# Rotation of queries and keys by position: halves of heads swapped by GpSimd's loads inside SBUF in place of rotation products on TensorE

## The reference, cut to what matters

```python
def apply_rope(x, cos, sin):
    xf = x.astype(jnp.float32)
    x1, x2 = jnp.split(xf, 2, axis=-1)
    c = cos[:, None, :]
    s = sin[:, None, :]
    return jnp.concatenate([x1 * c - x2 * s, x2 * c + x1 * s], axis=-1).astype(x.dtype)

def even_mixer(...):
    a_q, a_k, a_v, b_q, b_k, b_v, i_q, i_k, i_w = jnp.split(h @ w_in, EVEN_SPLITS, axis=-1)
    a_q = apply_rope(...cos64, sin64)      # and a_k: 8 heads of 64
    o_a = diff_attention(a_q, a_k, a_v, lam, subln, lambda_init)
    b_q = apply_rope(...cos64, sin64)      # and b_k: 8 heads of 64
    i_q = apply_rope(...cos32, sin32)      # 8 index heads of 32, and i_k: one of 32
    o_b = dsa_attention(b_q, b_k, b_v, i_q, i_k, i_w, topk)   # each query keeps its 64 best keys by index score
    return jnp.concatenate([o_a, o_b], axis=-1) @ w_out
```

## Time and profile before

| | |
|---|---|
| time, median of 3 runs | 1786.7 us (1786.68 to 1788.54) |
| the profiled execution's own time | 1785.52 us |
| its span | 1783.7 us |
| PE busy | 1715.3 us (96%) |
| DVE busy | 1159.3 us (65%) |
| ACT busy | 894.3 us (50%) |
| POOL busy | 7.4 us |
| the stretch from `idx` to the end of attention "even" | about 955 to 1080 us |

### The profile page before, as it was taken

The page is one execution under the profiler, slowest core; times in us unless marked ns, Lnnn a source line. Parts: engine busy times, 40 slices in busy tenths (PEclk is TensorE's granted clock), DMA queues, the critical chain, the costliest instruction groups (busy, mean ns, idle before and its releaser), DMA issues.

```text
span 1783.7 us, 22030 instructions
## 1 busy us (share of the span) xinstructions
PE 1715.3 (96%) x8926; PEld 1431.7 (80%) x8926; DVE 1159.3 (65%) x1613; ACT 894.3 (50%) x1271; POOL 7.4 (0%) x20
## 2 busy tenths in 40 slices
PE   5999999999989999999999989999999999999998
PEld 4798788888867888888888867888888889778887
DVE  7779888789766754565547967555655456675553
ACT  3555544465567444554444556444544445574432
POOL 0000000000000000000000000000000000000000
PEclk9999999999999999999999999999999999999999
DMA  8957677766624664555554324545555556345451
GB/s 355 401 228 274 266 298 289 297 253 245 259 77 186 234 224 177 200 197 177 185 195 178 119 71 177 182 169 192 201 188 177 184 207 225 116 153 182 169 192 47
DMA packets 54117, 363.43 MB, mean 204 GB/s; under 512 B 5744, under 2 KB 8944, under 8 KB 13056
## 3 DMA queue, kind: packets, MB, share of 16 engines
q1 hardware_dynamic: 52256, 351.47, 53.7%
q0 software_dynamic: 1760, 10.56, 1.5%
HBM read 360.95 MB, written 1.05 MB: 203 GB/s over the span
## 4 chain that ended last, share of the span: by engine, by line
PE 80%; DVE 12%; DMA 3%; ACT 3%; issue 1%; SPq 0%; POOL 0%; DVEq 0%; ACTq 0%
PE pp L603 77%; DVE low L1796 4%; DVE raw L1809 2%; DMA raw<-in_w 2%; PE pp L853 2%; DMA cst<-in_csts 1%; PE pp L785 1%; ACT wh L1270 1%; DVE hf L1940 1%; PE pp L930 1%; DVE tb L1796 1%; DVE x L1799 0%; DVE hl L1796 0%; DVE Sb L2091 0%; DVE sc L2192 0%
## 5 line engine op out<-in xcount | busy, mean ns | idle before, releaser
L1796 DVE TENSOR_TENSOR low<-raw,wh 128x2048 fp32r<-128x2048 f32 (+3 forms) x340 | 638.0, 1890 | 360.2 <-ACT wh L1270 359.8
L1270 ACT ACTIVATE wh<-raw 128x2048 fp32r<-128x2048 f32 (+3 forms) x346 | 536.1, 1567 | 436.3 <-PE pp L603 292.3
L603 PE MATMUL pp<-wh,hh 128*128 128x512 f32 x1312 | 522.0, 398 | 12.0 <-ACT hh L1300 6.7
L603 PE MATMUL pp<-low,hh 128*128 128x512 f32 x1312 | 514.6, 392 | 7.1 <-DVE low L1796 6.9
L603 PE MATMUL pp<-wh,hl 128*128 128x512 f32 x1312 | 507.3, 392 | 3.8 <-DVE hl L1796 3.8
L603 PEld LDWEIGHTS pp<-wh,hh 128*128 128x128 f32 x1312 | 247.7, 189 | 69.8 <-issue 16.0
L603 PEld LDWEIGHTS pp<-low,hh 128*128 128x128 f32 x1312 | 248.2, 189 | 58.6 <-DVE low L1796 9.8
L603 PEld LDWEIGHTS pp<-wh,hl 128*128 128x128 f32 x1312 | 247.6, 189 | 57.6 <-DVE hl L1796 5.1
L603 PE MATMUL pp<-wh,hidh 128*128 128x512 f32 x592 | 232.1, 392 | 0.0
L603 PE MATMUL pp<-low,hidh 128*128 128x512 f32 x592 | 230.6, 389 | 1.0 <-DVE low L1796 1.0
L603 PE MATMUL pp<-wh,hidl 128*128 128x512 f32 x592 | 230.6, 389 | 0.0
(11 more groups left out here) (207 smaller groups left out, 1159.6 us busy)
## 6 DMA issues: line engine op xcount, KB each, us to landing
raw<-in_w SPq DMA_DIRECT2D x314, 1024.0 KB, 4.8
raw<-in_w SPq DMA_DIRECT2D x24, 768.0 KB, 4.3
gain<-in_w POOLq DMA_DIRECT2D x6, 512.0 KB, 4.5
bT<-in_rel POOLq DMA_DIRECT2D x1, 2048.0 KB, 11.4
cst<-in_csts POOLq DMA_DIRECT2D x1, 1029.0 KB, 19.8
xT<-in_xT SPq DMA_DIRECT2D x1, 1024.0 KB, 7.4
binr<-in_bin POOLq DMA_DIRECT2D x1, 1024.0 KB, 10.9
wsT<-in_ws POOLq DMA_DIRECT2D x1, 1024.0 KB, 15.2
```

The costliest lines, as they stand in the source:

```text
L603: return e.matmul(out, lhsT, rhs, start=start, stop=stop, skip_group_check=True)
L1270: q.then_inc(e.activation(wh[j % NW][:, c], raw[i % NRAW][:, c], ACT.Copy), s_wh, (j, part))
L1796: return e.tensor_tensor(out, a, b, op)
```

## The change

The two rotation matrices leave the constants. The sine table takes the sign (minus in the first half of each head). PE's `rope` and its five calls are gone. POOL gets a function `turn_halves`: for each of the five groups it waits for ACT's copy, then moves each half of each head from `ta` to the place of the other half in `tb`, by one load inside SBUF for each block of partitions. That is 8 loads of 16 partitions x 3 KB for `idx`, and 4 loads of 32 partitions x 4 KB for each of the others, 24 in all. DVE's sine product reads `tb` in place of PSUM, in one instruction for all tiles, after it has waited for all loads of the group. On POOL the five calls stand between `gain_row("even_out", "dn2")` and `gain_row("dn3", "even_out")`.

```diff
-CSTS = [("ident", 128), ("bd64", 128), ("rot64", 128), ("rot32", 128), ("cos64", 256),
+CSTS = [("ident", 128), ("bd64", 128), ("cos64", 256),
         ("sin64", 256), ...
...
-        return np.cos(ang).astype(np.float32)[rows], np.sin(ang).astype(np.float32)[rows]
+        sign = np.where(p % d < d // 2, np.float32(-1), np.float32(1))[:, None]
+        return np.cos(ang).astype(np.float32)[rows], np.sin(ang).astype(np.float32)[rows] * sign
...
+        TURNS = {("idx", 0): (16, 3), ("aqk", 0): (32, 4), ("aqk", 1): (32, 4), ("bqk", 0): (32, 4), ("bqk", 1): (32, 4)}
+        s_turned = {key: signal("turned_%s%d" % key) for key in TURNS}
...
# tensor_program
-            def rope(key, kind, nt, ring):
-                q.wait_ge(s_sq, (key,))
-                small_tiles(key, ring, C("rot" + kind), ta.of((key,)),
-                            lambda n: tuple(range(2 * n, min(nt, 2 * n + 2))), (s_side, key))
...
             def idx_rest():
-                rope(("rope", "idx", 0), "32", 3, misc)
+                q.wait_ge(s_sq, (("rope", "idx", 0),))
...
-                if (qb, jj) == (1, 0):
-                    rope(("rope", "aqk", 0), "64", 4, misc)
...
-                if n == 1:
-                    rope(("rope", "aqk", 1), "64", 4, t_r)
...
-                    rope(("rope", "bqk", g), "64", 4, t_r)
...
# vector_program
-            def rope(name, gi, kind, nt, dst, scale, ring=misc):
+            def rope(name, gi, kind, nt, dst, scale):
                 key = ("rope", name, gi)
                 a = ta.of((key,))
-                s, before = tb.begin((key,), (s_side, key))
-                if before:
-                    q.wait_ge(*before)
+                s, _ = tb.begin((key,), (s_side, key))
                 q.wait_ge(s_sq, (key,))
                 q.wait_ge(s_side, ("tab", "sin" + kind))
                 q.then_inc(stt(dst, a[:, 0:nt, :], scale, bc4(rope_tab["cos" + kind], nt), ALU.mult, ALU.mult), s_side, (key, "cos"))
-                for n in range(2):
-                    w = min(2, nt - 2 * n)
-                    q.wait_ge(s_aux, (key, n))
-                    b = ring.of((key, n))[:, 0:256 * w].rearrange("p (m t) -> p m t", m=w)
-                    q.then_inc(stt(s[:, 2 * n:2 * n + w, :], b, scale, bc4(rope_tab["sin" + kind], w), ALU.mult, ALU.mult),
-                               s_side, (key, n))
-                q.wait_ge(s_side, (key, 1))
+                q.wait_ge(s_turned[name, gi], 0)
+                q.then_inc(stt(s[:, 0:nt, :], s[:, 0:nt, :], scale, bc4(rope_tab["sin" + kind], nt), ALU.mult, ALU.mult), s_side, (key, "sin"))
+                q.wait_ge(s_side, (key, "sin"))
                 q.then_inc(tt(dst, dst, s[:, 0:nt, :], ALU.add), s_side, key)
...
# pool_program
             gain_row("even_out", "dn2")
+
+            def turn_halves(name, gi):
+
+                key = ("rope", name, gi)
+                half, nt = TURNS[name, gi]
+                a, (s, before) = ta.of((key,)), (tb.of((key,)), tb.prior((key,)))
+                if before:
+                    q.wait_ge(*before)
+                q.wait_ge(s_sq, (key,))
+                for p in range(0, 128, half):
+                    o = p ^ half
+                    e.dma_start(s[p:p + half, 0:nt, :], a[o:o + half, 0:nt, :]).then_inc(s_turned[name, gi].sem, 16)
+
+            for name, gi in TURNS:
+                turn_halves(name, gi)
             gain_row("dn3", "even_out")
```

More of the change, by code:

```diff
@@ L157, in constants @@
     p = np.arange(128)
[L159 to L164, removed]
     def rope(d):
@@ L182, in constants @@
     made = {"ident": np.eye(128),
-            "bd64": (p[:, None] // 64 == p[None, :] // 64), "rot64": rot(64), "rot32": rot(32),
+            "bd64": (p[:, None] // 64 == p[None, :] // 64),
             "cos64": rope(64)[0], "sin64": rope(64)[1], "cos32": rope(32)[0], "sin32": rope(32)[1],
@@ L2222, in even_fill @@
                     yield
-                    rope("bqk", g, "64", 4, dst[:, :, :], scale, t_r)
+                    rope("bqk", g, "64", 4, dst[:, :, :], scale)
                 for qb in range(2):
@@ L2474, in vector_program @@
                 if n == 1:
-                    rope("aqk", 1, "64", 4, ak[:, :, :], 1.0, t_r)
+                    rope("aqk", 1, "64", 4, ak[:, :, :], 1.0)
             attention("even", units("even"), fill, even_rate, EVEN_NEEDS,
@@ L2567, in build @@
         s_ld["cst"].at = {0: 32}
+        for key, (half, nt) in TURNS.items():
+            s_turned[key].at = {0: 16 * 128 // half}
         s_out.at = {"all": 64}
```

## The result

Over 8 runs of each kernel the changed one takes 1795.7 us (1792.0 to 1801.2), the one before 1786.7 us. The ratio is 1.0049 (95% interval 1.0035 to 1.0062): slower by some 8.8 us, between 6.3 and 11. The profiled execution of the changed kernel took 1795.2 us with a span of 1793.4, against 1785.5 and 1783.7.

What follows compares the result with a forecast made beforehand. PE sets the pace at `idx` and `aqk` 0, DVE at the other three groups. Terms: -0.6 - 1.0 + 1.4 + 0 + 2.4 + 0.5 = +2.7 us, giving 1789.4; range 1784 to 1796.

Steps and rivals of the forecast that it cites:

- L: Time from issue to landing of a load inside SBUF, taken as 3.6 us from `gain`, bounded by 2.1 and 5.8.
- forecast case: Landing time between 3.0 and 4.2 us, chance 0.48, with a range of its own of 1787 to 1792 us.
- constants: Load of `cst` ahead of PE's first run: 128 KB fewer, so it lands earlier, a gain of 0.6 us.
- `idx` and `aqk` 0: First two groups: 1.8 us of `idx` products leave PE's stretch, 0.8 given back at `aqk` 0; gain 1.0 us.
- `aqk` 1: Keys `ak`: DVE stands still until the loads land at 996.9, a cost of 1.4 us.
- `bqk` 0: Group `bq`: loads land before DVE comes to the sine product, cost 0.
- `bqk` 1: Keys `bk`: DVE waits for loads landing at 1034.7, cost 2.4 us; PE waits some 7 us.
- PE's rival: Whole kernel: PE is the bound, so 8.7 us of products and 0.6 come back: 1777.4 us, chance 0.03.
- the collision: All turns: loads meet a megabyte of weights issued just ahead, landing takes 5.8 us, +10.6: 1797.3 us, chance 0.12.
- Short transfers: All turns: loads inside SBUF don't touch HBM and land in 2.1 us, -2.2: 1784.5 us, chance 0.22.
- DVE holds POOL up: POOL's loads wait for DVE's instruction, landing time up to 4.8 us, +6.3: 1793.0 us, chance 0.15.
- TensorE's clock: PE's new 3.2 us wait for `ak` may lower its clock; at most 1.1 us come through, taken as 0.5.

Runs made afterwards that it cites:

- `idx` alone: Only the `idx` group turned by loads, the other four by rotation products as in the kernel before: 1782.5 us, ratio 0.9982 to before.
- `warm_before`: The kernel before with 6 products that nobody reads added on PE ahead of `bk`: 1785.7 us, ratio 0.9995 to before.
- `aqk` 1 alone: Only the keys `ak` turned by loads, the other four groups by rotation products as in the kernel before: 1791.4 us, ratio 1.0020 to before.

## Why the prediction was right or wrong

The time, 1795.7, lies in the range, at its upper end. The sum was +2.7 us and the likeliest answer "the same"; measured is slower by 8.8. Most terms had the right sign, and the sum was 6 us short. That the range holds the result, by 0.3 us, is in part luck: L lies outside the forecast case (3.0 to 4.2), whose own range ended at 1792. Shifts in the stage, from the marks, changed kernel and its repeat:

| term | predicted | after | again |
|---|---|---|---|
| constants | -0.6 | -0.7 | |
| `idx` and `aqk` 0, to the end of `aq` | -1.0 | +0.2 | +0.4 |
| between `aq` and `ak` | 0 | +0.8 | 0.0 |
| `aqk` 1 | +1.4 | +2.9 | +2.4 |
| between `ak` and `bq` | +0.5 (clock) | +1.2 | +2.4 |
| `bqk` 0 | 0 | +0.1 | +0.3 |
| `bqk` 1 | +2.4 | +2.3 | +2.6 |
| tail | 0 | -0.9 | -0.5 |

- **Which engine bounds which group** was right. `idx` alone shifts everything by 1.87 us, as read from PE's stretch (1.8), its load is hidden, and PE doesn't wait for `ix`. The 19 tiles' 8.7 us came back nowhere else: PE's rival (1777.4) falls.
- **The constants** had the right sign; their size isn't shown. `cst` lands at 62.8 instead of 63.6, and PE's run starts 0.8 us earlier than in the earlier trace rows. But the issue moves from profile to profile, and `warm_before`, with all its constants, starts that run at 67.41. From issue to landing `cst` took 19.4 to 19.8 us in the nine profiles with the matrices and 19.1 to 19.4 in the five without, which makes some 0.3 us. Chain of waits of the changed kernel, 35 to 100 us:

```profile
43.68 19.14 DMA cst<-in_csts
...
65.12 2.30 DVE low L1783
...
67.46 32.56 PE pp L599 x206
```

- **The landing time L** is the first term that was mis-sized. Taken as 3.6 for every group, it is 4.4 to 4.6 for three and 3.1 for `bk`, at which only the tail of one weight load is under way; without weights beside it, it is 2.8 to 3.0. The reason given against the collision, that most of the megabyte has gone by when the last load is issued, was wrong: with the weights held back 1.4 us disappear for `aq` and 1.7 for `ak`. The rival's place and mechanism were right, its price of 5.8 was not. The estimate of 3.6 from the row `gain`, a median over other places, fits neither a load by itself nor one beside the weights.
- **POOL's first issue** was taken as right behind the copy. It comes 0.5 to 0.6 us later in all five turns (974.14 to 974.70 in the chain above). That was missing from the sum: with L at 4.4 and 0.5 of lag, `aqk` 0 gives -1.0 + 0.8 + 0.5 = +0.3 and `aqk` 1 gives 1.4 + 0.8 + 0.5 = +2.7. Both agree with the two profiles within 0.3 us. For `bqk` 1 the two errors cancel (3.1 instead of 3.6, and 0.5), so its +2.3 is right by luck.
- **Short transfers.** At L = 2.7 that rival gave about no change. The held-back weights made L = 2.7 and the stage is still +2.3. The prediction's own terms at L = 2.7, with the lag of 0.5 added, give -1.4 for `idx` and `aqk` 0, +1.0 for `aqk` 1 and +2.0 for `bqk` 1; measured are -1.3, +1.1 and +2.0, and +0.5 in the tail. So with the landing time and the lag right the account of DVE's waits comes out. The rival lacked the lag.
- **DVE holds POOL up.** POOL's loads are 0.48 us apart in every turn, beside a DVE with little pause, as the 0.53 of the earlier trace rows. No hold-up is seen between the loads. Whether the lag of 0.5 us ahead of the first has to do with DVE wasn't tried.
- **TensorE's clock** was mis-sized. The wait for `ak` came and lowered the clock as said, but "at most 1.1 us come through" was too low: 1.2 and 2.4 us in the two profiles, 2.2 with `aqk` 1 alone. The stretch from `ak` to `bq` shows it with the rivals away: it is back at 13.9 us in both kernels whose clock stayed at 1.00 behind `ak`. PE waited 4.3 and 4.0 us where the forecast had 3.2, and behind that wait it used up more than the 1.9 us of slack. The prediction also had no term for PE's wait for `rl`, 2.5 and 2.7 us, behind which the clock fell too, to 0.80 in one profile and 0.90 in the other; only the first has +0.8 between `aq` and `ak`, and whether the clock is the cause of that wasn't tried. And the lower level behind `bk`, taken as paid, became 0.5 to 0.9 us cheaper.

The terms add to +6.0 (6.7 of stage, less 0.7) and in the repeat to about +7, around the lower end of the interval of 6.3 to 11. The rest, 2 to 3 us of the 8.8, stays open: the scatter of the untouched first attention and of the stretch ahead of the first block is large enough for it in one profile, but the medians of both runs of the changed kernel show it, and no profile shows its place.

## What to carry to other kernels

Work can be taken from a busy TensorE and the time still get longer: look in the chain at each place for the engine that ends last, and move only those instructions to a transfer whose consumer is further away than the whole turn (here copy to landing 6.5 us, issue and lag included). A small load inside SBUF is to be priced with the large load that starts at the same moment, whose company took the landing from 2.7 to 4.4 us here. Where TensorE must wait for it, add what the lower clock costs behind the wait; here that was 1.2 to 2.4 us, beside 2.4 to 2.9 us for DVE's own wait.

## What was not expected of the hardware

- 128 KB inside SBUF take 2.7 us from issue to landing (median; 2.8 to 3.0 for the last of four) with the weights held back, and 4.4 beside the weights' 1 MB.
- GpSimd starts its first load 0.5 to 0.6 us after ScalarE's copy, for which it waited, has ended; further ones follow every 0.48 us. From ScalarE's queue each costs 0.70 us, and none lands earlier.
- Behind waits of nearly the same length (2.8 us) TensorE ran at 1.2 GHz for 6 us in one kernel and for 3.4 in another, and behind one of 2.7 us, for `ak` with the weights held back, not at all. With products that nobody reads in the wait it stayed at 2.4 GHz.
